# Squares in paired weight blocks: the MLP's first pairs at chunks 2, 6 and 10, the output projection's first blocks as a pair, a third square in the FFN's second pairs

## Time and profile before

| | us |
|---|---|
| median of three runs | 3221.59 |
| lowest, highest | 3221.43, 3221.6 |
| the profiled execution | 3220.65 |
| its span in the trace | 3218.9 |
| PE busy in the span | 3206.2 |
| DVE busy | 2287.8 |
| ACT busy | 1704.6 |
| POOL busy | 179.2 |

### The profile page before, as it was taken

How to read it: one execution, slowest core, us unless ns; L and a number is a source line. 1 busy time by engine, 2 the same in 40 slices (tenths; PEclk the granted TensorE clock), 3 DMA queues, 4 the chain that set the end, 5 groups by cost and what they waited for, 6 DMA issues and landing times.

```text
span 3218.9 us, 42110 instructions
## 1 busy us (share of the span) xinstructions
PE 3206.2 (100%) x16273; PEld 2721.0 (85%) x16273; DVE 2287.8 (71%) x2953; ACT 1704.6 (53%) x2394; POOL 179.2 (6%) x194
## 2 busy tenths in 40 slices
PE   9999999999999999999999999999999999999999
PEld 7888888888888888888988888888888888888887
DVE  6576568775686877777565677877786667787777
ACT  6555545454554545455454565545555746554454
POOL 1033100000000000001000200000010020000001
PEclk9999999999999999999999999999999999999999
DMA  8945666665666666666656556666666545666665
GB/s 268 255 126 158 176 188 197 202 215 184 184 195 196 193 194 188 203 188 192 198 166 191 170 178 189 189 198 189 185 202 192 179 155 180 188 192 197 188 189 173
DMA packets 325451, 611.00 MB, mean 190 GB/s; under 512 B 19708, under 2 KB 47176, under 8 KB 324640
## 3 DMA queue, kind: packets, MB, share of 16 engines
q1 hardware_dynamic: 321776, 596.15, 60.8%
q0 software_dynamic: 3504, 12.52, 1.5%
HBM read 605.32 MB, written 3.28 MB: 189 GB/s over the span
## 4 chain that ended last, share of the span: by engine, by line
PE 99%; DMA 0%; DVE 0%; SPq 0%; ACT 0%; issue 0%; DVEq 0%
PE ps L543 21%; PE ps L384 17%; PE ps L386 17%; PE ps L385 17%; PE ps L546 11%; PE ps L395 2%; PE ps L397 2%; PE ps L396 2%; PE ps L531 2%; PE ps L529 2%; PE ps L530 2%; PE ps L721 1%; PE ps L745 1%; PE ps L618 1%; PE ps L710 0%; PE ps L747 0%
## 5 line engine op out<-in xcount | busy, mean ns | idle before, releaser
L370 DVE TENSOR_TENSOR w_lo<-raw,w_hi 128x1024 fp32r<-128x1024 f32 (+2 forms) x1049 | 1256.3, 1238 | 359.2 <-ACT w_hi L359 341.3
L359 ACT ACTIVATE w_hi<-raw 128x1024 fp32r<-128x1024 f32 (+2 forms) x1049 | 1048.7, 1038 | 400.4 <-DMA raw<-ffn_up 77.2
L543 PE MATMUL ps<-l_both,w_hi 128*128 128x512 f32 x2944 | 934.0, 396 | 0.0
L546 PEld LDWEIGHTS ps<-l_both,w_lo 128*128 128x128 f32 x2944 | 553.2, 188 | 122.3
L546 PE MATMUL ps<-l_both,w_lo 128*128 128x256 f32 x2944 | 594.4, 278 | 0.0
L384 PE MATMUL ps<-w_hi,m_hi 128*128 128x512 f32 (+1 forms) x1212 | 469.6, 387 | 0.0
L386 PE MATMUL ps<-w_hi,m_lo 128*128 128x512 f32 (+1 forms) x1212 | 467.0, 385 | 0.0
L385 PE MATMUL ps<-w_lo,m_hi 128*128 128x512 f32 (+1 forms) x1212 | 466.4, 385 | 0.0
L543 PEld LDWEIGHTS ps<-l_both,w_hi 128*128 128x128 f32 x2944 | 456.1, 189 | 8.8
L384 PE MATMUL ps<-w_hi,l_both 128*128 128x512 f32 (+3 forms) x1168 | 447.6, 383 | 0.6 <-DVE l_both L643 0.6
L386 PE MATMUL ps<-w_hi,l_both 128*128 128x512 f32 (+3 forms) x1168 | 440.5, 377 | 0.0
(11 more groups left out here) (587 smaller groups left out, 3383.0 us busy)
## 6 DMA issues: line engine op xcount, KB each, us to landing
raw<-ffn_up SPq DMA_DIRECT2D x256, 512.0 KB, 3.7
raw<-w_in SPq DMA_DIRECT2D x175, 512.0 KB, 3.7
raw<-w_mlp_in SPq DMA_DIRECT2D x128, 512.0 KB, 3.7
raw<-w_mlp_out SPq DMA_DIRECT2D x128, 512.0 KB, 3.8
raw<-ffn_down SPq DMA_DIRECT2D x128, 512.0 KB, 4.2
raw<-ab_w_in SPq DMA_DIRECT2D x64, 512.0 KB, 3.6
raw<-w_branch SPq DMA_DIRECT2D x48, 512.0 KB, 4.0
raw<-cd_w_in SPq DMA_DIRECT2D x40, 512.0 KB, 3.8
```

Source lines behind the costliest of these rows:

```text
L359: nc.scalar.activation(w_hi[:, k % RING, 0:n], raw[:, k % RING, 0:n], ACT.Copy).then_inc(hi_done, 1)
L370: nc.vector.tensor_tensor(w_lo[:, k % RING, 0:n], raw[:, k % RING, 0:n], w_hi[:, k % RING, 0:n].bitcast(F32), ALU.subtract).then_inc(lo_do ...
L543: return nc.tensor.matmul(ps[:, banks[t], :], hi[:, j, P * t:P * (t + 1)], l_both[:, kt, :], start=opens, stop=stop)
L546: return nc.tensor.matmul(ps[:, banks[t], 0:TOK], lo[:, j, P * t:P * (t + 1)], lh[0][:, kt, :], start=False, stop=stop)
```

The core of the diff (the renumbering of counters is left out):

```diff
-        QUADS = ((2, 4, 8), (2, 4, 10))
-        M_ORDER = (tuple(range(NCH)), (0, 1, 2, 3, 5, 4, 6, 7))
+        QUADS = ((2, 6, 10), (2, 4, 10))
+        M_ORDER = ((0, 1, 3, 2, 5, 4, 6, 7), (0, 1, 2, 3, 5, 4, 6, 7))
...
-        F_QUADS, F_ORDER = ((4, 12), (6, 12)), ((0, 1, 2, 3, 4, 6, 5, 7), (0, 1, 3, 2, 4, 6, 5, 7))
+        F_QUADS, F_ORDER = ((4, 12), (6, 10, 12)), ((0, 1, 2, 3, 4, 6, 5, 7), (0, 1, 3, 2, 4, 5, 6, 7))
...
+        O_QUADS, O_ORDER, O_KT = (6, 12), (0, 2, 3, 1, 4, 6, 5, 7), (2, 10)
...
+            def mix_turn(k):
+                if k == 3:
+                    turn(pe, T_MIX + 3, mix[3], (merged, 9))
+                if k == 5:
+                    pe.wait_ge(lhs_ready, T_MIX + 4)
+            mm_pair(pe, Q_O, 0, U_O, 0, mh, O_QUADS, QT_O, QS_O, gate_sums, mlp_parts[1], need=(lhs_ready, T_MIX), evicted=U_O - 2, each=mix_turn,
+                    order=O_ORDER)
...
+            def pair_turns(c):
+                if c in (1, 3):
+                    n = c // 2
+                    turn(pe, T_O + n, xres[:, :, BW * n:BW * (n + 1)], (acc_free, U_O + 2), tp=tp_first)
...
+            mm_block(pe, Q_O + 2, U_O + 2, O_ACC[2], mh, each=pair_turns)
+            mm_block(pe, Q_O + 3, U_O + 3, O_ACC[3], mh, hook=third_turn)
+            pe.wait_ge(lhs_ready, T_O + 3)
...
+            k = O_QUADS[-1]
+            out_sum(0)
+            quad_sums_lo(dve, QS_O, gate_sums, 0, gate_raw)
+            quad_lo(dve, Q_O, 6, QT_O, mlp_parts[1], 6)
             turn_lo(dve, T_MIX + 3, tiles(mh, 12))
+            split_lo(dve, Q_O, range(8, k))
+            out_sum(1)
+            quad_sums_lo(dve, QS_O + 1, gate_sums, 1, gate_raw)
+            quad_lo(dve, Q_O, k, QT_O + 1, mlp_parts[1], 4)
+            split_lo(dve, Q_O, range(k + 2, 19))
+            quad_join(dve, 8 * Q_O + k + 2, U_O, 4, QP_O, QM_O, [[gate_rows[c][:, tt, :] for c in range(2)] for tt in range(2)], gate_v)
...
-                    if b == 3:
-                        quad_lo(dve, q + b, 12, QT_MLP + 6 * g + 1, mlp_parts, 8)
-                    else:
-                        split_lo(dve, q + b, (12, 13))
+                    split_lo(dve, q + b, (12, 13))
...
-                    split_lo(dve, qp, range(6, k))
+                    if p == 0:
+                        quad_lo(dve, qp, 6, QT_MLP + 6 * g + 1, mlp_parts, 8)
+                    split_lo(dve, qp, range(6 + 2 * (1 - p), k))
                     quad_lo(dve, qp, k, QT_MLP + 6 * g + 3 * p + 2, mlp_parts, 4)
                     split_lo(dve, qp, range(k + 2, 16))
                     quad_out(qp, u + 4 + 2 * p, p, g)
...
+                            quad_sums(dve, QS_F + 5 * layer + 2, ffn_a, ffn_b, ffn_s_raw)
+                            split_lo(dve, x, (o + 8, o + 9))
+                            quad_sums_lo(dve, QS_F + 5 * layer + 2, ffn_sums, 2, ffn_s_raw)
+                            quad_lo(dve, x, o + 10, QT_F + 7 * layer + 3, ffn_parts[layer][1], 8)
+                            quad_lo(dve, x, o + 12, QT_F + 7 * layer + 4, ffn_parts[layer][1], 4)
```

More of the change, by code:

```diff
@@ L630, in turn_hi, with turn_lo @@
             i.then_inc(thi_done, 1)
-        def turn_lo(dve, t, dst, gain=None, n=4):
+        def turn_lo(dve, t, dst, gain=None, n=4, tp=None):
+            src = tp4 if tp is None else tp
             if gain is None or n < 4:
@@ L635, in turn_lo @@
             if gain is None:
-                i = nc.vector.tensor_tensor(dst[1], tp4, dst[0].bitcast(F32), ALU.subtract)
+                i = nc.vector.tensor_tensor(dst[1], src, dst[0].bitcast(F32), ALU.subtract)
             else:
@@ L1054, in _ @@
                             load_x(k - 2)
-            for b in range(4):
+            for k in range(2 * NCH):
+                load_block(sp, Q_O, d["w_out"], 2 * P * O_ORDER[k // 2], BW * (k % 2), nch=1, k0=k)
+            for b in (2, 3):
                 load_block(sp, Q_O + b, d["w_out"], 0, BW * b)
@@ L1873, in _ @@
                 gate_unit(w)
+            k = O_QUADS[-1]
+            quad_sums_hi(act, QS_O, gate_sums, 0, gate_raw)
+            quad_hi(act, Q_O, 6, QT_O, mlp_parts[1])
             turn_hi(act, T_MIX + 3, tiles(mh, 12))
-            for b in range(4):
-                split_hi(act, Q_O + b, range(6, 12))
+            split_hi(act, Q_O, range(8, k))
+            quad_sums_hi(act, QS_O + 1, gate_sums, 1, gate_raw)
+            quad_hi(act, Q_O, k, QT_O + 1, mlp_parts[1])
+            split_hi(act, Q_O, range(k + 2, 19))
+            act.wait_ge(chunk_used, 8 * Q_O + k + 2)
+            act.wait_ge(acc_free, U_O)
+            nc.scalar.activation(gate_rows[0][:, 0, :], ps[:, 4, :], ACT.Copy).then_inc(p_copied, 1)
+            split_hi(act, Q_O, range(19, 22))
+            act.wait_ge(acc_free, U_O + 2)
+            for b in range(2):
+                squares(xres[:, :, BW * b:BW * (b + 1)], b, ssp, junk_x)
+            for b in range(2):
+                split_hi(act, Q_O + 2, range(6 + 2 * b, 8 + 2 * b))
+                turn_hi(act, T_O + b, tiles(lh, 4 * b), gains("norm_mlp")[:, 4 * b:4 * b + 4], tp=tp_first)
+            for b in (2, 3):
+                split_hi(act, Q_O + b, range(10 if b == 2 else 6, 12))
                 act.wait_ge(acc_free, U_O + b + 1)
@@ L2456, in _, with out_sum @@
                 gate_unit(w)
-            turn_lo(dve, T_MIX + 3, tiles(mh, 12))
+            def out_sum(n):
+                for dst, kt in ((gate_a, O_KT[n]), (gate_b, O_KT[n] + 1)):
+                    i = nc.vector.tensor_tensor(dst, mh[0][:, kt, :].bitcast(F32), mh[1][:, kt, :].bitcast(F32), ALU.add)
+                chain(i)
+                quad_sums(dve, QS_O + n, gate_a, gate_b, gate_raw)
+            k = O_QUADS[-1]
+            out_sum(0)
+            quad_sums_lo(dve, QS_O, gate_sums, 0, gate_raw)
+            quad_lo(dve, Q_O, 6, QT_O, mlp_parts[1], 6)
+            turn_lo(dve, T_MIX + 3, tiles(mh, 12))
+            split_lo(dve, Q_O, range(8, k))
[4 more added lines that the diff above has]
+            quad_join(dve, 8 * Q_O + k + 2, U_O, 4, QP_O, QM_O, [[gate_rows[c][:, tt, :] for c in range(2)] for tt in range(2)], gate_v)
+            dve.wait_ge(acc_free, U_O + 1)
+            for c in range(2):
+                dve.wait_ge(x_in[c], 32)
+                o = xres[:, :, BW * c:BW * (c + 1)]
+                i = nc.vector.tensor_tensor(o, gate_rows[c], o, ALU.add)
+            chain(i)
+            split_lo(dve, Q_O, (19,))
+            dve.wait_ge(chunk_used, 8 * Q_O + 16)
+            for c in range(2):
+                o = xres[:, :, BW * c:BW * (c + 1)]
+                i = nc.vector.tensor_tensor(o, ps[:, 2 * c:2 * c + 2, :], o, ALU.add)
+            i.then_inc(acc_free, 1)
+            split_lo(dve, Q_O, (20, 21))
             def add_x(q, u, b):
@@ L2464, in add_x @@
                 nc.vector.tensor_tensor(o, acc(O_ACC[b]), o, ALU.add).then_inc(acc_free, 1)
-            for b in range(4):
-                split_lo(dve, Q_O + b, range(6, 12))
+            for b in range(2):
+                split_lo(dve, Q_O + 2, range(6 + 2 * b, 8 + 2 * b))
+                turn_lo(dve, T_O + b, tiles(lh, 4 * b), gains("norm_mlp")[:, 4 * b:4 * b + 4], tp=tp_first)
+            for b in (2, 3):
+                split_lo(dve, Q_O + b, range(10 if b == 2 else 6, 12))
                 add_x(Q_O + b, U_O + b, b)
```

90 lines of the change are left out of this document (52 added, 38 removed).

## The result

| | us | runs |
|---|---|---|
| before, median (lowest to highest) | 3221.6 (3220.69 to 3223.46) | 16 |
| changed kernel, median (lowest to highest) | 3226.9 (3226.44 to 3231.37) | 16 |
| ratio, with its 95% interval | 1.0019 (1.0012 to 1.0025) | |
| forecast | 3227.8, range 3222.0 to 3230.5 | |

The medians are 5.3 us apart. The change makes the kernel slower by 0.19%, just inside the 0.2% that the forecast called "within".

A forecast was written before the change was run, and what follows sets the result against it. The prediction took PE to bound the kernel. Squares in output projection and FFN -2.4, MLP as a whole +8.4, output projection's wait +0.2: +6.2 us, 3227.8 us on the median; 8-in-10 range 3222 to 3230.5 us.

The forecast's parts named there:

- What bounds the kernel: Whole kernel: PE is busy for the whole span, so time is PE's work plus pauses too short for the page.
- The saving of a square: Output projection and FFN, two squares each: a square replacing two plain chunks gives back 0.60 us, 2.4 us in all.
- The old pause: MLP's first pair: PE's 0.39 us wait for DVE between two adjacent squares goes, four times, 1.6 us.
- The carried queue: MLP groups 1 to 3: DVE's full queue behind a later join holds p = 1's two squares, 2.9 us each group.
- The hand-over: Wherever PE waits for DVE: from DVE's end to PE's start, taken as 0.26 us.
- The pause that did not come: Output projection, before chunk 6: PE waits for DVE's last `m_lo`, 0.2 us lost.
- The FFN: FFN: DVE's sums are ready 4 and 2 us before PE wants them for its squares, so nothing is lost.
- The total: Whole kernel: the terms sum to +6.2 us, 3227.8 us on the median, 0.19% more.
- (a): Rival, MLP: DVE catches up, no new wait, all savings stay; -4.0 us, 3217.6 us; chance 0.06.
- (b): Rival, MLP: smaller wait from a sooner join or shorter sums; total moves 2.4 and more, 3219 to 3226; chance 0.12.
- (c): Rival, output projection: longer DVE chain before chunk 6, costing 3 us at its bound; 3228.1 to 3230.8 us; chance 0.16.
- (d): Rival, MLP: PE's pauses lower its clock, six held squares at 1.2 GHz; 29 us, 3257 us; chance 0.04.

The follow-up runs named there:

- after_again: The changed kernel as it is, profiled and timed once more with nothing changed: 3227.54 us, ratio 1.0020.

## Why the prediction was right

**What bounds the kernel.** PE did, before and after. All 6.0 us are found again as starts on PE, stage by stage.

**The saving of a square.** Forecast 0.60 us each. The output projection gave 1.09 for two, the FFN 0.58 in each layer. That is 2.25 us in place of 2.4; in part because a square of the output projection takes up to 4.87.

**The old pause.** Forecast 0.39 for each group; group 4, which has nothing else to lose, gave 0.34, and where the new waits were gone (p = 1 at 4, 8, 10) a group lasted 84.01 - 83.66 = 0.35 us less than before.

**The carried queue.** The step that decided everything, and each of its terms came out: the join began 949.39 - 917.46 = 31.93 us after p = 0 (forecast 31.9), lasted 5.05 (5.04), splits 2.27 (2.27), sums 963.31 - 956.71 = 6.60 (6.59), rows on `xres` 2.63 (2.64), sums 972.61 - 965.94 = 6.67 (6.67). They could be forecast so closely because none of these rows was new: all stood in the earlier trace rows, in this order and with next to no idle time between them. Only their start moved, and what the start would be came from the earlier trace rows. The first square was held 1.33 us (forecast 1.5), the second 1.66. A group lost 2.85 us (2.9).

**The hand-over.** This term was too large. From DVE's end to PE's start I took 0.26 us throughout. In the MLP it was 966.08 - 966.03 = 0.05 and 972.72 - 972.61 = 0.11, after which the second matmul came 0.1 late, so 0.15 to 0.2 us too much in each place. The 0.26 stands at the old pause only, in all four groups; what set it there is open.

**The pause that did not come.** Before chunk 6 of the output projection 0.2 us were forecast. The low part that PE needed there ended 16.98 us into the stage; the forecast had 16.96. But PE reached that place at 754.98 - 737.73 = 17.25 us and not at 17.11. Either this or a hand-over of 0.05 (it was 751.29 - 751.23 = 0.06 in the run with the extra row) is enough to remove the pause. The term was 0.2 us too large, small beside the MLP's 8.6.

**The FFN.** Nothing was lost, as forecast: 84.22 in both layers, where two squares at 4.85 for two pairs of chunks at 5.45 were all that was to be had. But the cover was forecast at 2 us for the last square, and it was 0.5 us in the first layer and 0.2 in the second. DVE had to wait for ACT's `w_hi` ahead of the two splits, which the forecast did not have. In the second layer (DVE twice, then PE) the last sums end at 2946.46 and PE wants them at 2946.66:

```profile
2930.30 2.36 DVE L373 TENSOR_TENSOR w_lo<-raw,w_hi 128x1024 fp32r<-128x1024 f32 x2 [1.65 <-ACT w_hi L362]
...
2944.10 2.36 DVE L485 TENSOR_TENSOR f_t_lo<-main,f_t_hi 128x1024 fp32r<-128x1024 f32 x2
...
2946.66 0.39 PE L398 MATMUL ps<-w_hi,m_hi 128*128 128x512 f32 x1
```

In `after_again` DVE was 0.3 us later still in its stage, and PE was held:

```profile
2941.24 2.36 DVE L485 TENSOR_TENSOR f_t_lo<-main,f_t_hi 128x1024 fp32r<-128x1024 f32 x2
...
2943.25 0.39 PE L400 MATMUL ps<-f_t_hi_b,f_s_lo 128*128 128x512 f32 x1
2943.70 0.47 PE L398 MATMUL ps<-w_hi,m_hi 128*128 128x512 f32 x1
```

DVE ends at 2943.60, PE was due at 2943.48 and starts at 2943.70. This is the 0.3 us of that run with the restart, and the same place cost 0.21 us in the run with the extra row and 0.13 in the one with the shorter join. That this stage came out to 0.04 us is in part luck.

**The total.** The stages say +6.0 us, the two sets of medians +5.3 and +6.5 (3227.54 - 3221.00). The forecast was +6.2. Of the 0.9 us by which the first pair of medians falls short of it, 0.2 is the terms above and the rest the scatter of medians.

**The rivals.** (a), no new wait, is what the kernels with squares at 4, 8, 10 or at 2, 6, 8 do: it needed another table. (b), a smaller wait, is what happens when the join shrinks or the second square moves: 3220.9 and 3222.1 us. (c) came within some 0.2 us of existing. (d), the clock: PE in stretches of 5 us around the two pauses (stretch, its length, PE busy, granted clock, DMA share, GB/s):

```profile
965.00:970.00 5.00, 3.92 (x17) 1.00 0.39 134
970.00:975.00 5.00, 3.49 (x16) 1.00 0.44 143
975.00:980.00 5.00, 5.00 (x24) 1.00 0.34 112
```

The granted clock stayed at its upper level, 2.4 GHz, through pauses of 1.3 and 1.7 us that lie 6 us apart, and the squares behind them last 4.9 to 5.0 us. They cost their own length and some 0.1 us of restart. But (d) was closer than this looks: in the same execution the idle time of 2.55 us at 127 us was followed by the lower level, for another 1.6 us. The Trainium skill ("TensorE: Matmul & The Clock Gate", section "Why this matters for your kernels") advises against idle gaps between bursts of matmuls, as they bring the lower clock. This trace agrees for the gap of 2.55 us and shows no fall for those of 1.33 and 1.66 us; no wait of a length in between was seen.

**What beats both kernels.** The changed kernel with p = 0's squares at 2, 6 and 8 (3217.67 us) or p = 1's at 4, 8 and 10 (3217.79): it keeps all that squares and the old pause give. Against before that is 3.3 us, 0.1%, at the edge of what the intervals tell; against the changed kernel it is some 9 us.

## What to carry to other kernels

Where an engine that is off the critical path runs its instructions in a fixed order, its idle time is only worth something behind the event that it waits for. DVE was 72% busy and idle for 3 us ahead of the join, yet a join that began 4 us later was paid for almost in full by PE, because behind it stood 23 us of work without a gap and two deadlines. So before an event is moved later, follow the queue behind it to the next idle time or the next deadline, whichever comes first; and spread deadlines (squares here) away from the place behind the event, as both of the faster tables do.

A forecast for such a move can be made to a tenth of a microsecond from the old trace, as long as the rows only shift. Where new rows come in that also wait for loads, as in the FFN, the same kind of sum was 2 us off. When two profiles are compared, compare stages and not spans: 4.6 of the 10.6 us between these two spans lay outside the stages that the change touches.

## What the runs showed of the hardware

- From the end of DVE's last row to the start of the PE that waits for it took 0.05 us behind rows on `xres` or `m_lo` and 0.10 to 0.11 us behind a square's low parts. It was the same whether PE had waited for 1.7 us or for 0.2 (FFN, second layer, `after_again`). In the old pause of the earlier trace rows it was 0.26 us, in all four groups; why isn't known. Then the second matmul comes some 0.1 us late.
- Rows of 128x512 on DVE that depend on the row just before follow at 0.72 to 0.83 us; with an independent row between them each takes its 0.60 to 0.66. Leaving out 2.6 us of rows saved 2.1.
- The granted clock stayed at 1.00 through two pauses of 1.3 and 1.7 us in 10 us. It went to 0.50 behind an idle time of 2.55 us, and PE, busy again, lost 1.6 us before it was back at 1.00. Slices of 81 us did not show it.
- One load of `w_in` near 127 us held PE for 2.55 us in one execution and for 0.60 in another of the same kernel; in three profiles of other kernels PE's starts there are 0.2 to 0.4 us late, in the rest they are not.
